# Heads in pairs, modulation blocks among the Fourier transforms, and two expert-gate rows on ScalarE: a change to a two-network kernel on one core

## The reference

```python
# attention, heads of 64; q and k are normalized per head and scaled by a gain
s = einsum('bqhd,bjhd->bhqj', q, k) / sqrt(64) + bias_or_mask     # (sink as one more column in layer 0)
p = softmax(s); o = einsum('bhqj,bjhd->bqhd', p, v)
# experts: each token has 8 heads x 16 picks (e1, e2) of 128 x 128 experts, with gates g
out = sum over picks of  gelu(x . u[e1,e2]) * g * v[e1,e2]
```

## Time and profile before

| | us |
|---|---|
| median of 3 runs | 2433.11 (2432.70 to 2433.71) |
| the profiled execution | 2433.73, its span 2431.9 |
| TensorE matmul busy | 2254.1 |
| VectorE busy | 1393.5 |
| ScalarE busy | 875.5 |
| GpSimd busy | 258.8 |

### The profile page before, as it was taken

How to read it: one execution, slowest core, us unless ns; L and a number is a source line. 1 busy time by engine, 2 the same in 40 slices (tenths; PEclk the granted TensorE clock), 3 DMA queues, 4 the chain that set the end, 5 groups by cost and what they waited for, 6 DMA issues and landing times.

```text
span 2431.9 us, 36361 instructions
## 1 busy us (share of the span) xinstructions
PE 2254.1 (93%) x13050; PEld 1880.3 (77%) x13050; DVE 1393.5 (57%) x2609; ACT 875.5 (36%) x1267; POOL 258.8 (11%) x269
## 2 busy tenths in 40 slices
PE   5999999999988998999899899986599999999998
PEld 2755478887876657999797678876589999999997
DVE  3555253433279463664577533988766666666665
ACT  3233132222253343433476201214444444444443
POOL 0033000000013151000000000019700000000000
PEclk8999999999989999999899899998899999999999
DMA  7247222223262244555543233330055555555553
GB/s 279 70 147 269 87 87 95 96 86 104 96 153 69 95 174 147 182 181 169 178 151 127 75 104 124 128 130 0 15 184 190 190 185 186 185 186 190 187 185 119
DMA packets 92840, 340.63 MB, mean 140 GB/s; under 512 B 10409, under 2 KB 10436, under 8 KB 92496
## 3 DMA queue, kind: packets, MB, share of 16 engines
q1 hardware_dynamic: 89280, 325.10, 39.7%
q0 software_dynamic: 3472, 14.35, 2.0%
HBM read 338.36 MB, written 1.05 MB: 140 GB/s over the span
## 4 chain that ended last, share of the span: by engine, by line
PE 77%; DVE 13%; ACT 3%; POOL 2%; issue 2%; DMA 1%; DVEq 1%; SPq 0%; POOLq 0%; ACTq 0%
PE bank L739 18%; PE bank L1014 14%; PE bank L1002 13%; PE bank L522 11%; PE bank L766 8%; PE bank L867 3%; DVE main_zone L1419 3%; DVE main_zone L1493 2%; POOL tail_zone L2047 2%; PE bank L981 2%; DVE first_w_parts L1422 1%; PE bank L710 1%; PE bank L691 1%; DVE tail_zone L1416 1%; PE bank L699 1%
## 5 line engine op out<-in xcount | busy, mean ns | idle before, releaser
L739 PE MATMUL bank<-act_parts,first_w_parts 128*128 128x512 f32 (+1 forms) x2928 | 560.7, 353 | 18.0 <-DVE act_parts L1419 17.3
L739 PEld LDWEIGHTS bank<-act_parts,first_w_parts 128*128 128x128 f32 x2928 | 474.5, 193 | 100.5 <-issue 17.5
L1422 DVE TENSOR_TENSOR first_w_parts<-weight_ring,first_w_parts 128x1024 fp32r<-128x1024 f32 x166 | 211.3, 1275 | 290.9 <-ACT first_w_parts L1160 290.4
L1014 PE MATMUL bank<-w_parts,a_parts 128*128 128x512 f32 x1536 | 370.7, 392 | 5.2 <-DVE a_parts L1422 4.7
L1422 DVE TENSOR_TENSOR w_parts<-weight_ring,w_parts 128x1024 fp32r<-128x1024 f32 x235 | 286.8, 1221 | 109.8 <-ACT w_parts L1160 109.8
L1014 PEld LDWEIGHTS bank<-w_parts,a_parts 128*128 128x128 f32 x1536 | 282.8, 189 | 60.4 <-issue 5.9
L1002 PEld LDWEIGHTS bank<-n_parts,w_parts 128*128 128x128 f32 x2568 | 322.1, 191 | 8.3
L1002 PE MATMUL bank<-n_parts,w_parts 128*128 128x256 f32 x2568 | 324.6, 283 | 0.0
L1160 ACT ACTIVATE w_parts<-weight_ring 128x1024 fp32r<-128x1024 f32 x235 | 247.9, 1056 | 196.8 <-PE bank L1002 159.1
L1160 ACT ACTIVATE first_w_parts<-weight_ring 128x1024 fp32r<-128x1024 f32 x166 | 175.0, 1057 | 247.7 <-PE bank L739 119.1
L522 PE MATMUL bank<-main_zone,weight_ring 128*128 128x256 f32 (+1 forms) x976 | 243.0, 411 | 1.4 <-DVE main_zone L1559 0.8
(11 more groups left out here) (216 smaller groups left out, 2120.0 us busy)
## 6 DMA issues: line engine op xcount, KB each, us to landing
weight_ring<-in_stream SPq DMA_DIRECT2D x618, 512.0 KB, 3.3
main_zone<-in_rel_bias POOLq DMA_DIRECT2D x6, 512.0 KB, 15.0
main_zone<-in_decay POOLq DMA_DIRECT2D x1, 1536.0 KB, 9.7
main_zone<-in_xT POOLq DMA_DIRECT2D x1, 1024.0 KB, 11.4
main_zone<-in_ctxT POOLq DMA_DIRECT2D x1, 1024.0 KB, 15.9
tail_zone<-in_rel_bias POOLq DMA_DIRECT2D x2, 512.0 KB, 26.1
tail_zone<-in_keysT POOLq DMA_DIRECT2D x1, 1024.0 KB, 5.2
out<-main_zone SPq DMA_DIRECT2D x2, 512.0 KB, 2.7
```

Source lines behind the costliest of these rows:

```text
L739: mm = pe.matmul(o[:, 0:w], wb[:, hw, k, :], fin[:, hx, k, 0:w], start=(k == 0 and n == 0), stop=(k == DC - 1 and n == 2))
L1014: mm = pe.matmul(acc[n][:, :], ap_[:, e % 3, ha, (n // 2) * P:(n // 2 + 1) * P], wp[(B + b) % PARTS][:, hw, (n % 2) * 512:(n % 2 + 1) * 51 ...
L1422: return dve.tensor_tensor(o, a, b, op)
```

## The change

Attention goes in 16 pairs a layer: two heads with the same queries and tile. The padded copies and their clears are gone. The scores are two matmuls over 64 partitions each, from the upper and lower half of the same tiles, into banks 0 and 1; the values are matmuls of 64 columns, the two heads in turns, whose results stand in the two halves of one bank and are copied at once. The factor 1/8 of the scores is multiplied into the gain of the queries at the start, so that VectorE only adds or copies; the maximum is negated in its reduction; scores are turned into exponentials in place, in four buffers. TensorE does the values of i-3 before the transposes of i-2. GpSimd's multiplication by the reciprocal has a second one, by 1.0.

Of the 48 modulation blocks of the first attention 16 go to the Fourier mixing (`EARLY`), six before its waits, two in each of rounds 3 to 7; each attention now has two a pair. The Fourier mixing takes banks 2 and 3 instead of 6 and 7, the rotations 0 and 1.

In the gates, of eight first rows VectorE makes four, ScalarE two, GpSimd two. ScalarE's: the square of (iota - e1), then max(0, g - g * square), which is g at the key and 0 elsewhere, as the next square is 1. It first negates keys and gates (128x256, once each). ScalarE's gate copies move behind by one iteration: those of the iteration before, then new rows.

```diff
-OWN1 = 5
+OWN1 = 4
+OWNP = 6
...
-        att_s = view(ATT0, 2, 520)
-        att_e = view(ATT0 + 1040, 2, 520)
-        att_pt = view(ATT0 + 2080, 2, 4, P)
+        att = view(ATT0, 4, 2, 514)
+        att_pt = view(ATT0 + 4 * 2 * 514, 2, 2, 4, P)
         mask_e = view(MASKE0, QT, T)
-        qpads = [view(V10, 2, 4, T), projections[1][:, 0:8, :].rearrange("p j (h n) -> p h j n", h=2)]
...
+            EARLY = 16
...
+                for f in fill[0][:6]:
+                    ada(*f)
                 pe.wait_ge(even_in, 16 * 4)
                 evacuated(pe, "ev_in", 10)
                 pe.wait_ge(qk_sums_read, QKN[0])
...
                         rotate(u - 3)
+                        for f in fill[0][2 * u:2 * u + 2]:
+                            ada(*f)
...
-                    if i >= 2:
-                        pe.wait_ge(scores_read, u0 + i - 1)
-                    pe.matmul(bank[i % 2][:, 0:n], qpads[l][:, half, qc, qt * P:(qt + 1) * P], pr[:, kc, T - n:T],
-                              start=True, stop=True).then_inc(scores_ready, 1)
+                    for half in range(2):
+                        if i >= 1:
+                            pe.wait_ge(scores_read, 2 * (u0 + i - 1) + half + 1)
+                        pe.matmul(bank[half][:, 0:n], pr[head(half), qc, qt * P:(qt + 1) * P], pr[head(half), kc, T - n:T],
+                                  start=True, stop=True).then_inc(scores_ready, 1)
 
                 def turn(i):
-                    pe.wait_ge(probs_ready, u0 + i + 1)
-                    if i >= 2:
-                        pe.wait_ge(pt_copied, u0 + i - 1)
-                    for kt in range(keys_of(l, us[i][1]) // P):
-                        mm = pe.transpose(bank[2 + i % 2][:, kt * P:(kt + 1) * P],
-                                          att_e[:, i % 2, kt * P:(kt + 1) * P], ident)
-                    mm.then_inc(pt_ready, 1)
+                    for half in range(2):
+                        pe.wait_ge(probs_ready, 2 * (u0 + i) + half + 1)
+                        if i >= 1:
+                            pe.wait_ge(pt_copied, 2 * (u0 + i - 1) + half + 1)
+                        for kt in range(keys_of(l, us[i][1]) // P):
+                            mm = pe.transpose(bank[2 + half][:, kt * P:(kt + 1) * P],
+                                              att[:, i % 4, half, kt * P:(kt + 1) * P], ident)
+                        mm.then_inc(pt_ready, 1)
...
-                    pe.wait_ge(pt_copied, u0 + i + 1)
+                    pair, qt = us[i]
+                    pe.wait_ge(pt_copied, 2 * (u0 + i) + 2)
                     if i >= 2:
                         pe.wait_ge(o_copied, u0 + i - 1)
                     n = keys_of(l, qt) // P
                     for kt in range(n):
-                        mm = pe.matmul(bank[4 + i % 2][:, 0:P], V[l][:, 4 - n + kt, 0 if l == 0 else pair, :],
-                                       att_pt[:, i % 2, kt, :], start=(kt == 0), stop=(kt == n - 1))
+                        for half in range(2):
+                            mm = pe.matmul(bank[4 + i % 2][head(half), 0:P], V[l][:, 4 - n + kt, 0 if l == 0 else pair, head(half)],
+                                           att_pt[:, i % 2, half, kt, :], start=(kt == 0), stop=(kt == n - 1))
...
+                for i in range(PAIRS + 3):
+                    if i < PAIRS:
                         scores(i)
-                        n = len(fill[l]) // GROUP
-                        for f in fill[l][i * n // UNITS * GROUP:(i + 1) * n // UNITS * GROUP]:
+                        for f in fill[l][(1 - l) * EARLY:][i * GROUP:(i + 1) * GROUP]:
                             ada(*f)
-                    if 0 <= i - 2 < UNITS:
+                    if 0 <= i - 3 < PAIRS:
+                        values(i - 3)
+                    if 0 <= i - 2 < PAIRS:
                         turn(i - 2)
-                    if 0 <= i - 3 < UNITS:
-                        values(i - 3)
...
                     if g % 2:
+                        pe.wait_ge(oh1_act, at(g // 2 + 1, 2))
                         pe.wait_ge(oh1_pool, at(g // 2 + 1, 2))
...
-                        act.wait_ge(rowmax_ready, u0 + i + 1)
-                        if i >= 2:
-                            act.wait_ge(pt_ready, u0 + i - 1)
-                        act.activation(att_e[:, i % 2, 0:n + 1], att_s[:, i % 2, 0:n + 1], ACT.Exp,
-                                       bias=stat[:, 1, u0 + i:u0 + i + 1],
-                                       accum_out=stat[:, 2, u0 + i:u0 + i + 1]).then_inc(exp_ready, 1)
+                        for half in range(2):
+                            u = 2 * (u0 + i) + half
+                            act.wait_ge(rowmax_ready, u + 1)
+                            e = att[:, i % 4, half, 0:n + (l == 0)]
+                            act.activation(e, e, ACT.Exp, bias=stat[:, 1, u:u + 1], accum_out=stat[:, 2, u:u + 1]).then_inc(exp_ready, 1)
...
+            act.wait_ge(picks_copied, 3)
+            for src, at in ((E1T0, NE1T0), (GT0, NGT0)):
+                act.activation(view(at, L), view(src, L), ACT.Copy, scale=-1.0).then_inc(negated, 1)
...
+            def first_rows(h, i=None):
+
+                def col(v, j):
+                    return v[:, j:j + 1] if i is None else v[:, bass.ds(i * 16 + j, 1)]
+                if i is not None:
+                    act.wait_ge(gate_psum, i * 4 + (2 * h - 2))
+                rows = one1[:, 8 * h + OWN1:8 * h + OWNP, :]
+                for m in range(OWNP - OWN1):
+                    last = act.activation(rows[:, m, :], iota, ACT.Square, bias=col(ne1, 8 * h + OWN1 + m))
+                last.then_inc(key_distance, 1)
+                act.wait_ge(key_distance, h + 1 if i is None else i * 2 + (h + 1))
+                for m in range(OWNP - OWN1):
+                    j = 8 * h + OWN1 + m
+                    last = act.activation(rows[:, m, :], rows[:, m, :], ACT.Relu, bias=col(gt, j), scale=col(ngt, j))
+                last.then_inc(oh1_act, 1)
+
+            def gates_out(h, i=None):
+
+                for g in (2 * h, 2 * h + 1):
+                    act.wait_ge(gate_psum, L // 4 - 3 + g if i is None else i * 4 + (g - 3))
+                    o = gates[:, AHEAD:, L - 16 + 4 * g:L - 12 + 4 * g] if i is None else gates[:, AHEAD:, bass.ds(i * 16 + (4 * g - 16), 4)]
+                    act.activation(o.rearrange("p e t -> p t e"), bank[g][:, :].rearrange("p (t e) -> p t e", t=4)[:, :, AHEAD:],
+                                   ACT.Copy).then_inc(gate_kept, 1)
+
+            for h in range(2):
+                first_rows(h)
+            with act.Fori(1, L // 16) as i:
+                for h in range(2):
+                    gates_out(h, i)
+                    first_rows(h, i)
+            for h in range(2):
+                gates_out(h)
...
-                    if l == 1 and j < 8:
-                        p, r = qpads[1][:, :, j, :], r.unsqueeze(1).broadcast_to([P, 2, L])
                     last = stt(p, p, par("qkg", g), r, ALU.mult, ALU.mult)
...
-                for half in range(2):
-                    h = slice(64 * half, 64 * half + 64)
-                    tt_(qpads[0][h, half], view(R0, 5, T)[h, 0:4], view(SQ0, 5, T)[h, 0:4], ALU.add)
-                tt_(projections[0][:, 8, :], view(R0 + 4 * T, T), view(SQ0 + 4 * T, T), ALU.add).then_inc(qk_ready, 1)
+                tt_(projections[0][:, 4:9, :], view(R0, 5, T), view(SQ0, 5, T), ALU.add).then_inc(qk_ready, 1)
...
+                for i in range(PAIRS + 3):
+                    if i < PAIRS:
+                        pair, qt = us[i]
                         n = keys_of(l, qt)
-                        if l == 0:
-                            dve.tensor_copy(s[:, n:n + 1], par("sink", pair + 4 * half))
-                            if n == T:
-                                last = stt(s[:, 0:T], b[:, 0:T], HD ** -0.5, mask_e[:, qt, :], ALU.mult, ALU.add)
+                        if i >= 4:
+                            dve.wait_ge(pt_ready, 2 * (u0 + i - 4) + 2)
+                        for half in range(2):
+                            u = 2 * (u0 + i) + half
+                            s = att[:, i % 4, half]
+                            b = bank[half]
+                            dve.wait_ge(scores_ready, u + 1)
+                            if l == 0:
+                                dve.tensor_copy(s[:, n:n + 1], par("sink", pair + 4 * half))
+                                if n == T:
+                                    last = tt_(s[:, 0:T], b[:, 0:T], mask_e[:, qt, :], ALU.add)
+                                else:
+                                    last = dve.tensor_copy(s[:, 0:n], b[:, 0:n])
                             else:
-                                last = ts(s[:, 0:n], b[:, 0:n], HD ** -0.5, None, ALU.mult)
-                        else:
-                            if i == 0:
-                                dve.wait_ge(bias_masked, 1)
```

(37 more changed lines are left out.)

124 lines of the change are left out of this document (54 added, 70 removed).

## The result

| | before | after |
|---|---|---|
| median of 4 runs, us | 2433.41 (2432.70 to 2433.83) | 2360.84 (2357.60 to 2362.61) |
| ratio | | 0.9701, 95% interval 0.9684 to 0.9717 |
| span of the profiled execution | 2431.9 | 2358.5 |

A forecast was written before the change was run, and what follows sets the result against it. TensorE's own order was taken to bound both attentions, GpSimd the gates (ScalarE after the change). Gains of 22.1, 2.2, 23.7 and 13.2, together 61.2, took 2433.1 to 2372 us; range 2355 to 2402, likeliest case 2358 to 2384.

The forecast's parts named there:

- Bound by TensorE's order in both attentions: Attentions: TensorE's own sequence sets the pace, 4.3 us a pair with 512 keys, 2.8 with 256; other engines keep up.
- The 0.3 for changes of shape: Attention pair on TensorE: three further changes of tile shape at 0.09 us each, 0.3 us.
- The lower ends for strips side by side: Attention pair: scores on two array halves run side by side, 0.95 us (above 1.81); values 1.1, between 0.9 and 1.78.
- Rival A: Attentions: the half tiles run one after the other, 5.8 us a 512-key pair, 2411 us in all; chance 0.16.
- Filling and emptying: Second attention: 1 us for first scores before 15 periods of 4.3, then 10.2 for the last pair's way through; 75.7.
- GpSimd's scaling: Attentions: multiplying 512 elements with two operations takes 1.56 us, bounds 1.3 to 2.3; 3.2 us a pair.
- Rival B: Attentions: GpSimd's two-operation scaling is slow, 2.3 us, 4.7 a pair; 2382 us in all; chance 0.10.
- Part 2: Modulation blocks among the Fourier transforms: first eight transforms gain 1.4 us, ten blocks cost 5.4, first attention begins 4.0 later.
- Part 3: Second layer's projection without padded queries: normalizing a query tile of 256 instead of 512 elements, eight times, gains 2.2 us.
- mask additions shift: Projection: bias loads start 3.5 us earlier, mask additions with them, slowing other VectorE instructions by the same amount: 0 +/- 2.
- Part 4: Expert gates: ScalarE becomes the bound, half iterations fall from 3.63 to 3.3 us; gain 13.2 us, bounds 6 to 17.
- Rivals C and D: Gates: C, halves back at 3.6 us, 2385, chance 0.08; D, table loads of 1283 ns, 2451, chance 0.03.

The follow-up runs named there:

- c1: The kernel after, but both score matmuls of a pair use the lower 64 partitions, the second head's scores left out: 2378.4 us, ratio 0.9774.
- v1: The kernel after, but a pair's value matmuls run head by head instead of the two heads in turns: 2369.7 us, ratio 0.9743.
- s1: The kernel after, but GpSimd multiplies by the reciprocal alone, without the second multiplication by 1.0: 2365.8 us, ratio 0.9730.
- g1: The kernel before with the change of the expert gates alone, attention and modulation as before: 2411.1 us, ratio 0.9912.
- m1: The kernel after, but GpSimd adds the mask to the biases in 16 pieces of 512 columns instead of 4 of 2048: 2353.3 us, ratio 0.9674.

## Why the prediction was right, and where its terms were off

The gain by spans, 73.4 us, is a fifth larger than the sum of 61.2, and the larger misses all lay on that side. What was said to bound each stage held; the sizes of several terms did not, and the stated range was wide enough for that.

**Bound by TensorE's order in both attentions: right.** The pair was forecast as 0.95 + 0.99 + 1.1 + 0.94 + 0.3 = 4.3 and is 1.06 + 1.00 + 1.02 + 1.02 = 4.10. The 0.3 for changes of shape stood beside terms that already held it: scores with the change are 1.06, transposes 1.02 instead of 2 x 0.47. The lower ends for strips side by side were right, and c1 shows that they hold only on different halves. Rival A is out. Of the 27.4 us in the second attention c1 takes back 10.3 and v1 7.3, and GpSimd's faster form alone was worth 8.2 in before. The new order of values and transposes, the four buffers and the smaller work of VectorE were not tried by themselves.

**Filling and emptying: wrong parts, near sum.** From the first scores to the last 58.9 us (806.58 to 865.45), not 65.5: the first three steps have no transposes or values. The way out takes 13.2, not 10.2. Together with the period these give 72.0 instead of 75.7.

**GpSimd's scaling: outside both bounds.** The step "bounds 1.3 to 2.3, I take 1.56, the row of the same size and place" failed. It took 0.69. A row of another form (comparison and multiplication at 128 elements, both operands from memory, 0.79) served as the nearest for the second operation, and a cheaper instruction with more work was not thought possible. The sum hardly suffered, since s1 costs only 5 us: the step erred where little hung on it. Rival B had its sign wrong.

**Part 2: right where the clock stays up.** The first transforms were to start at the full clock, and in after they did not (3.54 us), in s1 they did (1.97): the stage is 4.0 us longer than before where the clock stays up, as forecast, and 5.5 where it falls. "Start on an engine that has not idled" was wrong on its face, as 2.51 us of idle time stayed. The cover that the forecast named (the additions behind the last transforms) is there. The first attention, 61.9 for 62.5, was right.

**Part 3: 2.2 was right, 5.9 was chance.** The chain's period fell from 4.49 to 4.23 us. The stage takes 147.6 to 148.3 in seven kernels that share this code, 2.6 to 3.2 less than in before; in after it takes 145.0. (In g1, whose code is that of before in this stage, it took 149.4, so the 2.2 is borne out to about a microsecond, no closer.) In after the additions of the mask begin 48.7 us after the projection (710.29, 661.59), in s1 46.8, and hit two instead of four of VectorE's instructions, whose four in s1 are:
```profile
711.41 3.51 DVE L1464 SCALAR_TENSOR_TENSOR main_zone<-main_zone,small_zone 128x256 f32<-128x256 f32 x1
714.84 5.62 DVE L1467 TENSOR_TENSOR first_w_parts<-weight_ring,first_w_parts 128x1024 fp32r<-128x1024 f32 x1
...
723.07 2.12 DVE L1464 SCALAR_TENSOR_TENSOR main_zone<-main_zone,small_zone 128x256 f32<-128x256 f32 x1
725.11 5.57 DVE L1467 TENSOR_TENSOR first_w_parts<-weight_ring,first_w_parts 128x1024 fp32r<-128x1024 f32 x1
```
When they begin hangs on the bias loads (GpSimd waited 31.64 us for them in after, 29.72 in s1). The bound of 2 for "mask additions shift" was too narrow: m1 shows that the whole term is worth 7.

**Part 4: right bound, mis-sized.** ScalarE did become the bound, the range for the half (3.3) did not hold: 3.05. Copies were taken at their 0.90 us each, one behind the other; from start to start two take 1.44. Over 32 halves that is 8 us, of which some 3 go at the start, where ScalarE waits for the first products. The further 2.8 taken off for time lost at the low clock should not have been: with shorter halves the granted clock was 0.95 instead of 0.86, and the stage has no such loss. Stage 20.6 instead of 13.2, above the upper bound of 17. Rivals C and D are out: the trace of after has no table load in the loop; ScalarE's only gap in a half is the 0.17 for its own squares.

By spans the gain is 73.4, 12.2 us over the sum of 61.2: 7.4 in the gates, 3.7 in the second attention, 3.7 in the projection (about 3 of it chance in this profile of after), 0.5 in the first attention, less 1.5 in the transforms and 1.6 elsewhere.

## What to carry to other kernels

Price a group of instructions by the distance from start to start in a row of the same neighbours; durations of single ones overlap and were too long here by a fifth. Where two engines meet on one resource, the longest single instruction sets the price of each meeting: cut the one off the critical path into pieces. And when a change rests on two heads or tiles running side by side, look in the order of instructions for what stands next to what.
